# Splitting a mixer's weight unit into high and low parts in one pass instead of two halves

## What is computed

```python
# first block
z = h @ w_in
rg_x, rg_gate, q, k, v, g, f_low = jnp.split(z, splits, axis=-1)
# second block
proj = h @ w_in
c_q, c_kv, k_rope, q_m, k_m, v_m, o_m, i_m, f_m, g_mla, g_mlstm = jnp.split(proj, split_at, axis=-1)
```

## Time and profile before

| | |
|---|---|
| time, median of 3 runs | 2400.46 us (2397.96 to 2403.44) |
| the profiled execution | 2391.27 us, span of its core 2389.5 us |
| busy share of the span | PE 94%, weight loads 84%, DVE 74%, ACT 51%, POOL 2% |
| mean granted TensorE clock | 0.957 of full speed |
| the chain that ended last | PE 84%, DVE 8%, ACT 3%, DMA 2%, issue 2% |
| mixers of the first block | about 56 to 170 us and 415 to 540 us |
| mixers of the second block | about 1413 to 1646 us and 1901 to 2140 us |

### The profile page before, as it was taken

How to read it: one execution, slowest core, us unless ns; L and a number is a source line. 1 busy time by engine, 2 the same in 40 slices (tenths; PEclk the granted TensorE clock), 3 DMA queues, 4 the chain that set the end, 5 groups by cost and what they waited for, 6 DMA issues and landing times.

```text
span 2389.5 us, 33477 instructions
## 1 busy us (share of the span) xinstructions
PE 2254.6 (94%) x13955; PEld 2016.7 (84%) x13955; DVE 1776.4 (74%) x1895; ACT 1223.7 (51%) x1334; POOL 53.7 (2%) x101
## 2 busy tenths in 40 slices
PE   3989999987999999999999989999799999999997
PEld 2978999976888888888888888888799898888997
DVE  5977777866998988889889747777666664556675
ACT  2623443615767767677676636422455454324553
POOL 1000000000000000000000000000000000000000
PEclk9988999987999999999999979999899999999999
DMA  9747986754999999999999926747455264244551
GB/s 302 246 160 283 333 301 213 268 191 173 378 356 353 369 353 379 335 371 368 337 378 351 333 57 180 263 143 252 151 177 194 73 163 122 71 158 131 173 193 53
DMA packets 338896, 578.55 MB, mean 242 GB/s; under 512 B 48083, under 2 KB 208811, under 8 KB 326451
## 3 DMA queue, kind: packets, MB, share of 16 engines
q1 hardware_dynamic: 324041, 474.36, 58.5%
q0 software_dynamic: 13824, 100.67, 10.9%
q10 hardware_dynamic: 873, 1.31, 0.2%
HBM read 575.26 MB, written 1.05 MB: 241 GB/s over the span
## 4 chain that ended last, share of the span: by engine, by line
PE 84%; DVE 8%; ACT 3%; DMA 2%; issue 2%; SPq 1%; DVEq 0%; ACTq 0%; POOL 0%; POOLq 0%
PE bank L542 82%; ACT arena L1417 1%; DVE w_low L1898 1%; SPq L432 1%; DMA ring<-in_w_in 1%; DVE ada_acc L1906 1%; PE bank L1196 1%; DVE arena L1906 1%; DMA ada_in<-in_ada_w 1%; DVE arena L1898 1%; ACT mix_hi L1417 1%; DVE arena L2344 1%; DVE arena L2101 1%; DVE h L1906 0%; DMA ring<-in_ffn_w_up 0%
## 5 line engine op out<-in xcount | busy, mean ns | idle before, releaser
L1898 DVE TENSOR_TENSOR w_low<-ring,moe_w_hi 128x2048 fp32r<-128x2048 f32 x264 | 594.4, 2285 | 14.6 <-ACT moe_w_hi L1417 14.2
L1417 ACT ACTIVATE moe_w_hi<-ring 128x2048 fp32r<-128x2048 f32 x264 | 505.5, 1917 | 156.7 <-DMA ring<-in_moe_w 99.7
L542 PE MATMUL bank<-moe_w_hi,hx_hi 128*128 128x512 f32 (+1 forms) x768 | 285.2, 378 | 2.0 <-DVE hx_low L1898 2.0
L542 PE MATMUL bank<-moe_w_hi,hx_low 128*128 128x512 f32 (+1 forms) x768 | 284.1, 376 | 0.0
L542 PE MATMUL bank<-h_hi,w_hi 128*128 128x256 f32 x1056 | 262.7, 287 | 10.7 <-ACT h_hi L1417 6.9
L542 PE MATMUL bank<-mix_h_hi,mix_hi 128*128 128x256 f32 (+2 forms) x848 | 254.8, 301 | 14.1 <-DVE w_low L1898 5.0
L542 PE MATMUL bank<-h_hi,w_low 128*128 128x256 f32 x1056 | 261.6, 284 | 0.0
L542 PE MATMUL bank<-mix_h_hi,w_low 128*128 128x256 f32 (+2 forms) x848 | 248.6, 293 | 0.0
L542 PE MATMUL bank<-h_low,mix_hi 128*128 128x256 f32 (+2 forms) x848 | 242.6, 292 | 0.0
L1417 ACT ACTIVATE arena<-bank 128x512 f32<-128x512 f32 (+2 forms) x174 | 91.3, 525 | 268.0 <-PE bank L542 264.6
L542 PEld LDWEIGHTS bank<-h_hi,w_hi 128*128 128x128 f32 x1056 | 202.1, 191 | 12.4 <-issue 8.0
(11 more groups left out here) (190 smaller groups left out, 4403.3 us busy)
## 6 DMA issues: line engine op xcount, KB each, us to landing
ring<-in_moe_w SPq DMA_DIRECT2D x264, 1024.0 KB, 6.2
ada_in<-in_ada_w POOLq DMA_DIRECT2D x96, 1024.0 KB, 7.5
ring<-in_w_in SPq DMA_DIRECT2D x56, 1024.0 KB, 5.4
ring<-in_ffn_w_up SPq DMA_DIRECT2D x44, 1024.0 KB, 7.7
ring<-in_ffn_w SPq DMA_DIRECT2D x33, 1024.0 KB, 6.8
ring<-in_ffn_w_down SPq DMA_DIRECT2D x22, 1024.0 KB, 4.9
ring<-in_w_out SPq DMA_DIRECT2D x16, 1024.0 KB, 5.5
ring<-in_w_br_mla SPq DMA_DIRECT2D x4, 1024.0 KB, 5.0
```

What stands on the lines that cost most here:

```text
L542: ins = nc.tensor.matmul(out, lhsT, rhs, start=start, stop=stop, skip_group_check=shared)
L1417: return nc.scalar.activation(out, in_, f, **kw)
L1898: return nc.vector.tensor_tensor(out, a, b, op)
```

## The change

A unit is now copied in one ACT instruction and subtracted in one DVE instruction over all its columns; PE waits for the low part once, at the start of the unit; the semaphore `half_used` is gone, and ACT waits for the whole use of the unit that held the buffer before. The flow of loads, the order of units and PE's matmuls stay as they are.

```diff
         def split_parts(key):
-            n = KB // 2 * unit_width(key)
-            return plan[key][0], mix_hi[split[key][0] % 2], (slice(0, n), slice(n, 2 * n))
+            return plan[key][0], mix_hi[split[key][0] % 2], slice(0, KB * unit_width(key))
...
                     def third(kb):
-                        done = {KB // 2 - 1: "half_used", KB - 1: "units_used"}.get(kb) if i == blocks - 1 else None
+                        done = "units_used" if i == blocks - 1 and kb == KB - 1 else None
                         mm(out, hi[:, kb, c], h_low[:, kb, :], start=False, stop=(kb == KB - 1), inc=done)
                     for kb in range(KB):
-                        if i == 0 and kb % (KB // 2) == 0:
+                        if i == 0 and kb == 0:
                             need("split_lo")
...
             def high(key):
-                slot, hi, halves = split_parts(key)
-                there = split[key][1]
+                slot, hi, cols = split_parts(key)
                 act.wait_ge(slot_full[slot], 16 * plan[key][1])
-                for half, cols in enumerate(halves):
-                    if there and there[0] in SPLIT and half == 0 and unit_width(there) >= unit_width(key):
-                        act.wait_ge(s["half_used"], split[there][0] + 1)
-                    elif there:
-                        used(there)
-                    func(hi[:, cols], ring[:, slot, cols], ACT.Copy).then_inc(s["split_hi"], 1)
+                if split[key][1]:
+                    used(split[key][1])
+                func(hi[:, cols], ring[:, slot, cols], ACT.Copy).then_inc(s["split_hi"], 1)
...
             def low(key):
-                slot, hi, halves = split_parts(key)
-                for cols in halves:
-                    need("split_hi")
-                    tt(w_low[:, slot, cols], ring[:, slot, cols], hi[:, cols].bitcast(F32), ALU.subtract)\
-                        .then_inc(s["split_lo"], 1)
+                slot, hi, cols = split_parts(key)
+                need("split_hi")
+                tt(w_low[:, slot, cols], ring[:, slot, cols], hi[:, cols].bitcast(F32), ALU.subtract)\
+                    .then_inc(s["split_lo"], 1)
```

More of the change, by code:

```diff
@@ L94 @@
 moe_hid moe_turned moe_ht_hi moe_ht_lo moe_hx_psum moe_hx_hi moe_gather_in moe_prep moe_spread_t
-moe_spread moe_added dn_down moe_y moe_y_low routing_psum logits_sb dn_psum z_up mla_sb half_used
+moe_spread moe_added dn_down moe_y moe_y_low routing_psum logits_sb dn_psum z_up mla_sb
 """
@@ L603, in tokens_split @@
                     for kb in range(KB):
-                        if tb == 0 and kb % (KB // 2) == 0:
+                        if tb == 0 and kb == 0:
                             need("split_lo")
-                        done = {KB // 2 - 1: "half_used", KB - 1: "units_used"}.get(kb) if tb else None
+                        done = "units_used" if tb and kb == KB - 1 else None
                         mm(out, mix_h_hi[:, kb, tokens], low[:, kb, :], start=(kb == 0), stop=False)
```

## The result

| | before | after |
|---|---|---|
| median of 9 runs each | 2397.5 us | 2406.87 us (2401.35 to 2413.5) |
| ratio of the runs | | 1.0053, 95% interval 1.0038 to 1.0067 |
| span of the profiled execution | 2389.5 us | 2403.2 us |
| mean granted TensorE clock | 0.957 | 0.956 |

The change makes the kernel slower by 0.53%, that is 12.7 us (9.1 to 16.1) on 2397.5. The ratio is not the quotient of the two medians, which are 9.4 us apart (1.0039); that quotient lies inside its interval. The profiled executions differ by 13.7 us.

A forecast was written before the change was run, and what follows sets the result against it. PE was taken to bound the kernel. Four stages, 1.0 + 2.2 + 3.6 + 4.1, and 1.7 for the clock give 12.6 us; on 2400.46 that is about 2413 us, range 2404 to 2421.

The forecast's parts named there:

- What bounds the kernel: PE, 94% busy and 84% of the chain; a unit reaching PE later costs time one for one.
- What is removed: Fewer passes save DVE 0.07 and ACT 0.08 us per full unit, together 0.4 us on the chain.
- First block, layer 0: Later start of `q` +0.8 and hand-over of copies +0.3, less saved passes: sum +1.0 us (0.6 to 1.3).
- First block, layer 1: `q` starts 1.92 us later, `g` 0 adds 0.2, less 0.1 for saved passes: +2.2 us (1.8 to 2.8).
- Case (b): Start where ACT's copy stands directly in front of DVE's subtraction: PE waits 1.07 + 0.85, together 1.92 us more.
- Second block, layer 1: `cq` 0 and `ckv` +2.8 in all, `gmla` 3 and `gml` 1 +0.66 each: sum +4.1 us (2.8 to 4.3).
- Second block, layer 0: `cq` 0 and `ckv` +2.8, `gmla` 3 +1.07, `gml` 1 absorbed, saved passes -0.3: +3.6 us (2.5 to 4.9).
- The clock: One stretch at 1.2 GHz after the 2.9 us idle before `q`, first block, layer 1: +1.7 us.
- The experts: Sign against the forecast: stages between mixers (575 to 1377 us) changing by more than 1 us, meaning another cause.
- rival 2: More low clock, at `ckv` stalls, attention gaps of layer 1 and later in the first block: +19 to +23; 0.08.
- rival 3: Waits absorbed by slack behind the starts; only the second block's starts count, about 2404 us; chance 0.12.
- Rival 4: Faster: passes saved on the chain outweigh; with all 56 units on the chain -8.4 us, 2392; chance 0.03.

The follow-up runs named there:

- convolution moved away: Passes PE waited on moved ahead in the queues: with the change's whole passes (ckv in halves) 0.9998, with the earlier kernel's halves 0.9987, both against the kernel before.
- the start alone: Kernel before, but PE waits for both low halves before a unit's first matmul; passes and hand-over stay by halves: 1.0048.
- both: Kernel before, still two passes per unit, but ACT waits for whole use of the buffer and PE for both low halves: 1.0021.
- the subtraction whole: Kernel before, but DVE subtracts a unit in one pass and PE starts when it is done; ACT copies in halves: 1.0044.
- second measurement: The changed kernel itself run again, against the kernel before, on one chip with the moved kernels: 2408.43 us, 1.0055.
- the kernel with moves and halves: Kernel before, halves kept everywhere, with the passes PE waited on moved ahead in the queues: 0.9987, then 0.9971 when repeated.
- selective kernel: The change for 54 units, with halves and half hand-over kept for the ten units whose starts were predicted to cost: 0.9993.

## Why the prediction was right, and where it was not

**What bounds the kernel**: right. PE's lateness came through one for one where PE had been waiting for the first half, but for the absorbed starts of the second block's layer 0 (below).

**What is removed**: 0.07 and 0.08 us per full unit, as taken; 54 saved passes bring 0.9993 (0.9973 to 1.0013). The Trainium skill, Perfetto Trace Analysis, Optimizing Scalar/DVE Operations, states that breaking up instructions may let work be completed sooner where ACT and DVE cause bubbles on other engines. The runs agree: whole passes everywhere 1.0053, ten units in halves 0.9993.

**Later starts, by stage**, from the steps of the table without the clock's:
- *First block, layer 0*, +1.0 forecast: 0.71 and 0.32, 1.03.
- *First block, layer 1*, +2.2 forecast: 1.92 and 0.31, 2.23. The idle of 2.90 is the forecast's 2.9. Case (b) knows only ACT's copy in front of DVE's pass. With the convolution moved away, whole passes and halves still lie 1.92 apart (0.78 and -1.14), now because both passes begin only at whole use of the buffer. Hand-over by itself would hardly do it: an estimate from the rows, 0.04 + 1.07 + 0.03 + 1.22 + 0.14 = 2.5 us from whole use to PE with halves, is just inside the 2.7 that PE works meanwhile. It takes whole passes and whole hand-over together; no run has moved halves with whole hand-over. The number was right, the cause incomplete, and that the two causes are of one size is chance.
- *Second block, layer 1*, +4.1 forecast: 1.06, 1.77, 0.67 and, for `gmla` 3, about the same again, since of its 2.13 some 1.5 is the clock's. Together 4.2.
- *Second block, layer 0*, +3.6 forecast: this step failed in part. `cq` 0 and `ckv` came as forecast (idle 0.48 to 1.54, and 1.77). But `gmla` 3's 1.07 did not arrive. Before the change PE had three idle times in this stretch, 1.02 in the earlier trace rows and these two (timeline of PE of the kernel before):

```profile
1557.90 0.52 PE L913 MATMUL bank<-const,arena 128*128 128x128 f32 x3 [1.66 <-DVEq L1893]
1559.48 0.84 PE L542 MATMUL bank<-arena 128*64 128x128 f32 x6 [1.07 <-ACTq L1412]
```

  They are 3.75 together. After, they are 1.07 at `gmla` 3, 1.06 at `gml` 1 and 1.66, 3.79 together: the two new waits took the place of 1.02 and 1.07. The forecast read one absorbing wait, gave it to `gml` 1, and stopped; the next two rows held another of the same size. So +2.9 instead of +3.6. In all five profiles with whole starts and the old order (the change twice, the start alone, both, and the subtraction whole) PE's idle time from `gmla` 3 to `gml` 2 is longer than before by no more than 0.04 to 0.26.

The four together are 10.3 to 10.4, forecast 10.9. This is near the 10.1 us by which PE's idle time grew, and inside the intervals of both measurements.

**The clock**, +1.7 forecast. Behind `q` of layer 1 it came as forecast: 3.4 us at 1.2 GHz, which cost 1.49 (2.58 in the second profile). Stretches that were not forecast lie behind `q` of layer 0 (`k` 1.57 and 1.58 later in the two profiles; in the kernel before the stretch lay on `flow`, one unit earlier, where `q` followed without idle time), and behind `cq` 0 of layer 1 of the second block, after 1.91 (`cq` 1 starts 1.49 and 1.48 later). Each profile has one that the other lacks: the first behind `gmla` 3 of layer 0, after an idle of only 1.07, the second behind `cq` 0 of layer 0, after 1.91. Later in the attention the kernel before had low stretches which the changed one lacks. Over the span the clock's records hold 207 us at the lower level before and 212 in either profile of the change, half of which is work lost: +2.8 us, and PE is busy 3.6 us longer. So in the profiles the term was 1 to 2 us too small. Over the runs it isn't shown at all: those of the second measurement have a mean granted clock of 0.955, the kernel before 0.952. It is also the part that the kernel doesn't own: the thirteen profiles hold from 207 to 254 us, the two of the kernel with moves and halves 214 and 224.

**The experts**, where a change of more than 1 us was to mean another cause. PE's stretch on them took 2.1 us longer in the first profile and 2.6 in the second. They begin inside a stretch of low clock which lasts 5.2 us into them, 3.8 before; that is 0.7 us. The rest, 1.5 and 1.9, lies in a few short waits, where PE turns the hidden rows of an expert and DVE's product comes late (waits of PE from 578 to 1381.3 in the first profile, then from 584.4 to 1388.2 in the second; before there was none):

```profile
PE bank L1195 <- DVE arena L1893: 0.8, 2, 0.4
```

```profile
PE bank L1195 <- DVE arena L1893: 1.5, 2, 1.1
```

They stand at 925.8, 1228.4 (0.11, too short for the list) and 1329.7 in the first, at 630.9 and 1235.9 in the second, and put PE back by 1.6 and 1.9. In front of DVE is ACT, which empties the bank late behind a copy of expert weights; in four of the five cases that copy had waited for a DMA. The other kernels, whose experts are the same code, have one or two such waits each, of 0.1 to 0.4 us, at changing experts, and are 0.3 to 0.9 us longer less the clock's part. So it is known what the time is, but not whether the change makes it longer: its two profiles are 0.6 and 1.0 us beyond what varied by itself.

**The sum.** 12.6 us were forecast, the pairs of runs give 12.7 (9.1 to 16.1) and the second measurement 13.2. Against the profile's 13.7 it was 0.6 too much in the steps and 1 to 2 too little for the clock, which partly cancel, and it had no term for the experts. The absolute time, 2413, is 6 us over the median: 3 because the kernel before ran at 2397.5 in these runs and not at 2400.46, 3 because the medians are 9.4 us apart. Of rival 2 (more low clock) stretches came true that it had not named, behind `q` of layer 0 and `cq` 0 of layer 1 in both profiles; the stalls of 1.61 at `ckv` brought none in either profile. Of rival 3 absorption came true in one layer, for both starts there. Rival 4 did not occur: the selective kernel saves almost all the passes, and its interval ends at -6.5 us, short of the -8.4 of that rival.

## What to carry to other kernels

Splitting a producer's pass in two costs a fixed sum per piece (here 0.07 to 0.08 us) and gives the consumer its start earlier by a whole piece (1.07 to 1.92 us), so decide it unit by unit: halves or quarters at the few starts for which the bottleneck engine waits, and it hardly matters anywhere else. For a buffer that is handed over, compare the chain from last use to first use (here 4.4 us) with the bottleneck's work on the unit between; only where that is short, as at `ckv` behind half a unit or `q` behind `flow`, does handing over by halves count, and here only together with whole passes (with half passes alone `ckv` lost nothing). And when a wait is to be absorbed by idle time behind it, list all the idle rows up to the next point that the engine cannot make up, not the first one alone.

## What was not expected of the hardware

The same idle time led to different clocks. Two kernels have an idle of 2.11 us at the same place. The timelines of PE, of the kernel with the start alone and then of the one with both edits in halves:

```profile
438.91 0.36 PE L555 MATMUL bank<-mix_h_hi,mix_hi 128*128 128x256 f32 x1 [2.11 <-DVE w_low L1912]
439.10 0.30 PE L555 MATMUL bank<-mix_h_hi,w_low 128*128 128x256 f32 x1
439.22 0.40 PE L555 MATMUL bank<-h_low,mix_hi 128*128 128x256 f32 x1
439.42 0.42 PE L555 MATMUL bank<-mix_h_hi,mix_hi 128*128 128x256 f32 x1
```

```profile
439.70 0.36 PE L555 MATMUL bank<-mix_h_hi,mix_hi 128*128 128x256 f32 x1 [2.11 <-DVE w_low L1912]
439.90 0.28 PE L555 MATMUL bank<-mix_h_hi,w_low 128*128 128x256 f32 x1
440.01 0.28 PE L555 MATMUL bank<-h_low,mix_hi 128*128 128x256 f32 x1
440.13 0.28 PE L555 MATMUL bank<-mix_h_hi,mix_hi 128*128 128x256 f32 x1
```

In the first, matmuls start 0.20 us apart from the third on, at 1.2 GHz, and the next unit is 1.49 late; in the second they start 0.12 apart throughout. So here a wait of about 2 us costs its own length, and another 1.5 us on top in some executions. Even 1.07 us of idle, at `gmla` 3 of layer 0, had such a stretch behind it in one profile of the change and none in the other.
